# Latent heads: the next head's scores ahead of this head's transposes, with two probability buffers; first loads, first down block and program end reordered

## The reference

```python
for l in range(DEPTH):                        # DEPTH = 2, D_MODEL = 1024
    n = rms_norm(x, attn_norm[l])
    h = n @ w_in[l]                           # 1472 columns: group A q k v, latent q, latent kv, rope key
    q_b = (rms_norm(h[q_lora], q_norm) @ w_uq).reshape(b, s, 4, 128 + 64)
    ckv, k_rope = rms_norm(h[kv], kv_norm), rope(h[kr])
    o_a = window_attention(q_a, k_a, v_a, sinks)             # group A: 8 heads, banded
    # group B, 4 latent heads; prompt, chunk-causal over 512 keys
    s = (q_nope_h . (ckv @ w_uk_h) + q_rope_h . k_rope) * scale
    o_h = softmax(mask(s)) @ (ckv @ w_uv_h)
    # the samples attend in latent space to 256 cached latents + 16 new ones
    x = x + concat(rms_norm(o_a), rms_norm(o_b)) @ w_out
    n = rms_norm(x, ffn_norm[l])
    x = x + (silu(n @ w_gate) * (n @ w_up)) @ w_down         # D_FF = 2816 = 22 tiles of 128
y = rms_norm(x, final_norm)
```

## Time and profile before

| | us |
|---|---|
| runs, median of 3 | 1589.42 (1586.65 to 1590.17) |
| the profiled execution | 1587.84 |
| its span, first to last instruction | 1586.5 |
| PE busy / DVE busy / ACT busy / POOL busy | 1473.4 / 943.1 / 667.4 / 167.4 |
| PE waits in the latent heads, layer 0, 186 to 264 us | 14.5 |
| mean granted TensorE clock over the span | 0.965 of full |

### The profile page before, as it was taken

The page is one execution under the profiler, slowest core; times in us unless marked ns, Lnnn a source line. Parts: engine busy times, 40 slices in busy tenths (PEclk is TensorE's granted clock), DMA queues, the critical chain, the costliest instruction groups (busy, mean ns, idle before and its releaser), DMA issues.

```text
span 1586.5 us, 23820 instructions
## 1 busy us (share of the span) xinstructions
PE 1473.4 (93%) x9510; PEld 1386.9 (87%) x9510; DVE 943.1 (59%) x1579; ACT 667.4 (42%) x1302; POOL 167.4 (11%) x114
## 2 busy tenths in 40 slices
PE   5987888899999999999999788899999999999997
PEld 4877666799899999999988666668998999999997
DVE  5267535475878467467534754446677765765763
ACT  4255535333335235235334464353343542532543
POOL 3024200220000000000111440011100000000004
PEclk9998989799999999999999888998999999999999
DMA  3222012023222322321222201121312231332212
GB/s 142 81 80 69 14 48 63 27 80 93 78 75 94 89 74 81 97 64 54 75 81 90 75 25 40 42 69 44 103 54 87 81 110 51 99 98 64 88 41 100
DMA packets 150605, 115.74 MB, mean 73 GB/s; under 512 B 14656, under 2 KB 142912, under 8 KB 150464
## 3 DMA queue, kind: packets, MB, share of 16 engines
q1 hardware_dynamic: 150496, 114.23, 23.7%
HBM read 109.43 MB, written 6.62 MB: 73 GB/s over the span
## 4 chain that ended last, share of the span: by engine, by line
PE 75%; DVE 12%; ACT 6%; issue 3%; POOL 2%; DMA 1%; SPq 0%; ACTq 0%; DVEq 0%; POOLq 0%
PE ps L524 28%; PE ps L1086 9%; PE ps L1085 9%; PE ps L1087 9%; PE ps L571 2%; PE ps L573 2%; PE ps L572 2%; ACT whi L1152 1%; DVE wlo L1600 1%; PE ps L885 1%; PE ps L911 1%; PE ps L798 1%; PE ps L872 1%; DMA wraw<-w_uq 1%; PE ps L693 1%
## 5 line engine op out<-in xcount | busy, mean ns | idle before, releaser
L1600 DVE TENSOR_TENSOR wlo<-wraw,whi 128x1024 fp32r<-128x1024 f32 (+2 forms) x120 | 127.3, 1061 | 221.2 <-ACT whi L1152 220.9
L1152 ACT ACTIVATE whi<-wraw 128x1024 fp32r<-128x1024 f32 (+2 forms) x120 | 109.1, 914 | 260.1 <-PE ps L524 164.9
L1086 PE MATMUL ps<-tl,ringh 128*128 128x320 f32 x576 | 177.8, 309 | 0.0
L1087 PE MATMUL ps<-tth,ringl 128*128 128x320 f32 x576 | 177.5, 308 | 0.0
L1085 PE MATMUL ps<-tth,ringh 128*128 128x320 f32 x576 | 177.0, 307 | 0.0
L524 PE MATMUL ps<-hh,whi 128*128 128x320 f32 x704 | 161.1, 310 | 6.5 <-DVE hl L1928 3.5
L524 PE MATMUL ps<-hh,wlo 128*128 128x320 f32 x704 | 160.4, 309 | 0.0
L524 PE MATMUL ps<-hl,whi 128*128 128x320 f32 x704 | 160.3, 309 | 0.0
L1086 PE MATMUL ps<-tbl,ringh 128*128 128x320 f32 x432 | 133.5, 309 | 0.0
L1087 PE MATMUL ps<-tbh,ringl 128*128 128x320 f32 x432 | 133.4, 309 | 0.0
L1085 PE MATMUL ps<-tbh,ringh 128*128 128x320 f32 x432 | 133.4, 309 | 0.0
(11 more groups left out here) (368 smaller groups left out, 3345.0 us busy)
## 6 DMA issues: line engine op xcount, KB each, us to landing
raw_gate<-w_gate SPq DMA_DIRECT2D x18, 1024.0 KB, 5.3
raw_up<-w_up SPq DMA_DIRECT2D x18, 1024.0 KB, 5.4
wraw<-w_down SPq DMA_DIRECT2D x48, 384.0 KB, 3.5
wraw<-w_in SPq DMA_DIRECT2D x16, 512.0 KB, 3.8
wraw<-w_out SPq DMA_DIRECT2D x32, 128.0 KB, 2.9
wraw<-w_out SPq DMA_DIRECT2D x16, 256.0 KB, 3.1
wraw<-w_gate SPq DMA_DIRECT2D x8, 512.0 KB, 3.9
wraw<-w_up SPq DMA_DIRECT2D x8, 512.0 KB, 4.0
```

The costliest lines, as they stand in the source:

```text
L1086: mm(o, wh[:, c, :], xl[:, c, :], start=False, stop=False, skip_group_check=True)
L1087: ins = mm(o, wl[:, c, :], xh[:, c, :], start=False, stop=c == KH - 1, skip_group_check=True)
L1152: run(whi[:, slot(s, unit_width(u))], wraw[:, slot(s, unit_width(u))], ACT.Copy).then_inc(unit_hi.sem, 1)
L1600: vec.tensor_tensor(wlo[:, w], wraw[:, w], whi[:, w], ALU.subtract).then_inc(unit_lo.sem, 1)
```

## The change

Six parts, with names as in the code:

1. **Heads.** A second probability buffer pm1; heads use pm and pm1 by turns. Scores take three banks, blocks 0 and 1 sharing bank 0, and the four blocks become three groups (`rows_of`), so that p_max needs one reduction for two blocks. PE's order for each h is now p_scores(h+1), p_turn(h), k_nope(h+2), q_nope(h+2), p_values(h). The transposes go to three banks (4; 5; 3, in the last head 7), so no copy stands between two of them.
2. **Before the heads.** k_nope(1) comes ahead of p_scores(0); the samples' transposes take four banks; latent_values stands right behind them; the splitting of w_uv moves to the input stage (after unit 10), its load behind unit 9's.
3. **Start.** Of kc only the identity is loaded first (64 KB), the rest after unit 1 of w_in; SP's wait for n_lo, with gv and the masks, comes after unit 4. The high and low parts of unit 0 are made before the last token tile is copied out, those of unit 1 after chunk 2, and the masks' copy leaves the start on DVE.
4. **First down block.** wraw, whi and wlo are cut so that four of its 512-column units fit; up to six are loaded and split ahead. PE does rows 0 to 2 of d = 0 and of d = 1, and only then row 3 of both. Some of DVE's preparation comes later. SP waits, before each of these loads, until the one before in the same semaphore has landed.
5. **Layer boundary.** The wait for n_lo moves in both layers; the rest of the layers' seam stays.
6. **End.** The gain is multiplied into yT ahead of the transposes (ACT for chunks 0 to 6, in place of nh; DVE for chunk 7), ten transposes come ahead of the last unit, the last squares are added by PE in PSUM, and ACT and DVE write the scaled tiles at once. fg, its load and POOL's seven instructions go.

```diff
@@ SP
-        sp.dma_start(kc[:, :], a["consts"][:, 0:K_W]).then_inc(consts_in.sem, 16)
+        sp.dma_start(kc[:, 0:P], a["consts"][:, 0:P]).then_inc(consts_in.sem, 16)
...
+                if U_DOWN < u < U_DOWN + NC_:
+                    sp.wait_ge(raw_in[s].sem, raw_value(s, l, u) - 16)
...
-                if u == 1:
+                if u == 9:
+                    sp.dma_start(uv[:, :, :], w_uv[l]).then_inc(uv_in.sem, 16)
+                if u == 1 and l == 0:
+                    sp.dma_start(kc[:, P:K_W], a["consts"][:, P:K_W]).then_inc(tables_in.sem, 16)
+                if u == 4:
                     if l == 0:
                         sp.dma_start(mask_in[:, :], a["consts"][:, K_W:]).then_inc(win_in.sem, 16)
                     sp.wait_ge(n_lo.sem, n_lo.at(l, 1))
@@ PE, the heads
             for h in range(BH):
                 if h + 1 < BH:
-                    k_nope(h + 1)
-                p_turn(h)
-                if h + 1 < BH:
                     p_scores(h + 1)
                 else:
+                    pe.wait_ge(p_e.sem, p_e.at(l, 3 * BH - 1))
                     sample_queries()
-                    c_turn(0)
-                if h == 0:
-                    latent_values()
-                p_values(h)
+                p_turn(h)
                 if h + 2 < BH:
+                    k_nope(h + 2)
+                    pe.wait_ge(p_tact.sem, p_tact.at(l, h + 1))
+                    pe.wait_ge(p_tdve.sem, p_tdve.at(l, 2 * h + 2))
                     q_nope(h + 2)
                 if h == BH - 1:
-                    c_turn(1)
+                    c_turn(0)
+                p_values(h)
+            c_turn(1)
@@ PE, block 0
+                    if blk == 0 and d == 1:
+                        down_rows(blk, d, range(TILES[blk] - 1))
+                        for both in range(2):
+                            down_rows(blk, both, [TILES[blk] - 1]).then_inc(unit_used.sem, 1)
+                        continue
@@ ACT, the exponentials
-            def p_exps(h):
-                for i in range(TS):
+            def p_exp(h, k):
+                act.wait_ge(p_nm.sem, p_nm.at(l, 3 * h + k + 1))
+                if h >= 2 and k == 0:
+                    act.wait_ge(p_t.sem, p_t.at(l, 3 * h - 3))
+                for i in rows_of[k]:
@@ DVE, the end
-            vec.scalar_tensor_tensor(out=yout[:, t, 512:D], in0=ps[:, 2 * (t % 3) + 1, :], scalar=rs[:, t:t + 1], in1=fg[:, 512:D],
-                                     op0=ALU.mult, op1=ALU.mult).then_inc(y_dve.sem, 1)
+            vec.tensor_scalar(yout[:, t, 512:D], ps[:, (6 if t == 3 else 2 * (t % 4)) + 1, :], rs[:, t:t + 1], None, ALU.mult).then_inc(y_dve.sem, 1)
@@ POOL, the end
-        for t in range(NT):
-            pool.wait_ge(y_scaled.sem, t + 1)
-            add(yout[:, t, 0:512], yout[:, t, 0:512], fg[:, 0:512], ALU.mult).then_inc(y_pool.sem, 1)
```

More of the change, by code:

```diff
@@ L400, in load @@
                     parts, k, w = src.shape
-                    dst = wraw[part0:part0 + parts, s * SLOT + first * width:s * SLOT + (first + k) * width]
+                    c0 = unit_cols(u).start + first * width
+                    dst = wraw[part0:part0 + parts, c0:c0 + k * width]
                     dst = dst.rearrange("p (k n) -> p k n", k=k)[:, :, 0:w]
@@ L485, in _ @@
                 first, end = GROUPS_OF[blk]
-                load_down(blk, 0)
-                load_down(blk, 1)
+                ahead = 2 if blk else 6
+                for d in range(ahead):
+                    load_down(blk, d)
                 if blk == 0:
@@ L515, in unit_parts @@
         def unit_parts(u, n):
-            s = unit_slot(u)
-            return [w[:, slot(s, unit_width(u))].rearrange("p (k n) -> p k n", n=n) for w in (whi, wlo)]
+            return [w[:, unit_cols(u)].rearrange("p (k n) -> p k n", n=n) for w in (whi, wlo)]
         def by_weights(outs, w, k, cols, xh, xl, first, last):
@@ L532, in sums, with y_turn @@
             ins.then_inc(stat_sum.sem, 1)
+        def y_turn(t, chunks):
+            banks = 6 if t == 3 else 2 * (t % 4)
+            for c in chunks:
+                ins = turn(ps[:, banks + c // 4, (c % 4) * P:(c % 4 + 1) * P], yT[:, c, tok(t)], ident)
+            return ins
         def spread(n, bank):
@@ L873, in p_turn @@
+                for bank, rows in ((4, (0,)), (5, (1, 3)), (3 if h < BH - 1 else 7, (2,))):
+                    for j in rows:
+                        o = 384 if j == 3 else 0
+                        for i in range(j, TS):
+                            ins = turn(ps[:, bank, o + (i - j) * P:o + (i - j + 1) * P],
+                                       pms[h % 2][:, POFF[i] + j * P:POFF[i] + (j + 1) * P], ident)
                     ins.then_inc(p_t.sem, 1)
             def p_values(h):
-                pe.wait_ge(p_tact.sem, p_tact.at(l, 2 * h + 2))
+                pe.wait_ge(p_tact.sem, p_tact.at(l, h + 1))
@@ new lines, in _ @@
+        for t in range(NT):
+            mm(ps[:, 7, 500 + t:501 + t], ssq[:, tok(t)], one, start=True, stop=False, skip_group_check=True)
+            if t == 0:
+                pe.wait_ge(sq_new.sem, sq_new.at(DEPTH, 1))
+            ins = mm(ps[:, 7, 500 + t:501 + t], sq[:, 1, tok(t)], one, start=False, stop=True, skip_group_check=True)
+        ins.then_inc(stat_sum.sem, 1)
+        pe.wait_ge(stat_sd.sem, stat_sd.at(DEPTH, 1))
+        y_turn(3, range(NC_)).then_inc(tile_turned.sem, 1)
+        pe.wait_ge(y_scaled.sem, 1)
@@ L1151, in weight_hi @@
             act.wait_ge(unit_used.sem, unit_used.at(l, used_before(u)))
-            run(whi[:, slot(s, unit_width(u))], wraw[:, slot(s, unit_width(u))], ACT.Copy).then_inc(unit_hi.sem, 1)
+            run(whi[:, unit_cols(u)], wraw[:, unit_cols(u)], ACT.Copy).then_inc(unit_hi.sem, 1)
         act.wait_ge(consts_in.sem, 32)
@@ L1207, in _ @@
                         run(v[:, :, :], hm[:, :, C_V:C_Q], ACT.Copy).then_inc(v_new.sem, 1)
+                if u == 10:
+                    act.wait_ge(uv_in.sem, uv_in.at(l, 16))
+                    run(uvh[:, :, :], uv[:, :, :], ACT.Copy).then_inc(uv_hi.sem, 1)
                 if u == 8:
@@ L1380, in _ @@
                 if h + 1 < BH:
[L1381 to L1390 removed]
+                    p_exp(h + 1, 0)
+                    p_exp(h + 1, 1)
                 else:
@@ L1685, in _ @@
                     latents_norm()
+                if u == 10:
+                    dve.wait_ge(uv_hi.sem, uv_hi.at(l, 1))
+                    vec.tensor_tensor(uvl[:, :, :], uv[:, :, :], uvh[:, :, :], ALU.subtract).then_inc(uv_lo.sem, 1)
             def keys_out_dve(t):
```

363 lines of the change are left out of this document (204 added, 159 removed).

## The result

The changed kernel takes 1533.95 us (median of four runs, 1531.5 to 1534.86), the kernel before 1588.74 us on the same chip: a ratio of 0.9654, 95% interval 0.9637 to 0.967. It is 55 us faster where 44 were forecast, and lies a hair under the stated range (1534 to 1562). The profiled execution has a span of 1532.6 us, so the two traces differ by 53.9 us.

A forecast was written before the change was run, and what follows sets the result against it. PE, busy 1473.4 of 1586.5 us, was taken as the bound, with only gaps and half-clock stretches to win: heads 31.2, start 6.3, block 0 4.6, end 2.1, sum 44.2; from 1587.84 to 1543.6, plus 1.6 for the median: 1545 us, range 1534 to 1562.

The forecast's parts named there:

- the clock of the heads: Latent heads: of 7.0 and 8.6 us lost to the clock, 1.9 and 3.5 won, 5.1 a layer left in place.
- Rival B: Clock stays up through the latent stage (+10 us) and unit 2 is ready in time (+3): 1533 us; chance 0.15.
- rival C: Gaps between short groups keep PE at half clock through the latent stage, 51 us a layer more: 1647 us; chance 0.02.
- Heads, gaps: Latent stage: PE's gaps fall from 14.5 to 1.6 us, 12.9 a layer; a middle head takes 11.5 us.
- Start: Input stage: unit 2 lands early, PE resumes at 34.35 instead of 40.65 us, still at half clock; gain 6.3 us.
- Block 0: First down block: three gaps, 3.3 us a layer, go; waits of 0.3 and 0.7 us remain; gain 4.6 us in all.
- End: Final stores: reciprocal 0.7 us earlier, first store moves from 1578.70 to about 1576.6 us; gain 2.1 us.
- A: Heads close only halfway, each waiting 1.5 us for qnl or p_norm; they give 18 us, not 31: 1558 us; chance 0.20.
- D: Scores of h+1 can't run ahead; only start, block 0 and end give, 13 us: 1576 us; chance 0.06.

The follow-up runs named there:

- values_early: Changed kernel with the samples' values straight behind the samples' transposes, ahead of latent_values; 1534.64 us.
- before_k: Kernel before with one move, k_nope(1) ahead of the scores of head 0; 1583.43 us, ratio 0.9976 to the kernel before.
- one_buf: Changed kernel with one buffer of probabilities instead of two, PE's order unchanged; 1542.86 us, ratio 0.973 to the kernel before.
- end_old: Changed kernel with the old end (gain on POOL and DVE, all transposes behind the last unit); 1534.83 us, ratio 0.9661 to the kernel before.
- end3: Changed kernel, ten transposes moved behind the last unit, sums over chunks 0 to 6 right behind its product, one start for the bank; 1531.49 us, ratio 0.9641.
- end2: Changed kernel, ten transposes moved behind the last unit, sums over chunks 0 to 6 right behind its product, a start per column; 1530.66 us, ratio 0.9653.

## Why the prediction was right and wrong

**The step that failed** is the one on the clock of the heads: "The small matmuls stay and a small gap ahead of the first scores stays, so I leave these 5.1 in place and count only the others as won." All of it was won: 15.0 us by the granted clock (which is given to two digits, so some 0.5 us either way in each layer) instead of 5.4. That is about the whole miss of 9.7, 53.9 against 44.2; the errors of the other terms about cancel. The scores of head 0 ran at full clock behind the 0.8 us that stayed, and so did the samples' values. I had taken the 64-column matmuls for the cause, since they stood at 0.56 in the earlier trace rows. The same matmuls ran at 1.00 in the changed kernel, at 1.00 behind a wait of 1.35 us (values_early), and at both levels in one execution of before_k. They were where the fall showed, not what made it. What went with every fall in this stage was standing still: by the granted clock, one wait of 2.2 us put back cost 1.7 us in layer 0 and nothing in layer 1, two cost 3.5 and 1.7, and the row of waits of the kernel before 6.9 and 8.0. But not every standstill took the clock, and by what rule some do stays open.

Rival B had this mechanism, at a chance of 0.15 and 1533 us, and the argument against it was the same misreading. That the time fell so near its 1533 is in part luck: of its 13 us, the 3 for unit 2 in time did not come (PE still waited 2.37 us), and in their place stand the 1.8 us that block 0 gave beyond its forecast and the 1.6 us that had been added for the median, which now lies 0.3 us under the profiled execution.

A second misreading stands beside it: "1.00 in the middle heads of before" is true of the head in the earlier trace rows, but in layer 1 one ran at 0.51 for 3.4 us (before_k, above). It was used against rival C. Rival C's own condition is off too: 22 us a layer are lost by spending 44 us at half clock, not 22.

**Heads, gaps** (25.8 forecast, 24.1 measured): the mechanism was right and the size near. The 0.8 ahead of the scores and the copies of ptm ahead of p_values(2) (0.94) came where they were forecast; 0.29 ahead of p_values(3) had been missed. A middle head takes 10.97 us and not 11.5, since it had been sized by PE's busy time in a stretch with pauses.

The Trainium skill (TensorE: Matmul & The Clock Gate, section A second HAM failure mode: psum-queue depth-cycling) tells of a kernel in which frequent short pauses between groups of matmuls made the clock swing between its levels. The kernel before agrees in part (0.93 and 0.92 over its stages, with the row of waits). The changed middle heads have no pause (10.97 of 10.97 us busy) and can't show it, and one_buf has waits of 0.7, 0.7 and 2.1 us at 1.00.

**Start** (6.3, 7.1): the mechanism held, step by step. nl(7) ended at 33.8 and not at 32.4, wlo(2) at 34.96 and not at 34.3, so unit 2 began 5.7 us earlier; the rest of the 7.1 came behind it, where the kernel before restarted at half clock. "The restart at half clock stays" was wrong for this trace: behind 2.37 us PE started at full clock, behind 7.73 and 6.61 at half. It was right for end_old and end3, at half behind 2.04 and 2.11 us.

**Block 0** (4.6, 6.4): the mechanism was right, the size low. Of the two residual waits of 0.3 and 0.7 only one of 0.32 came, and PE's busy time fell by 0.3 us a layer with the waits, at a clock of 1.00 in both.

**End** (2.1, 0.7): the sum left out that the squares of chunk 7, now added by PE, double the sums, from 1.17 us to 2.3. The reciprocal came 0.5 us later and not 0.7 earlier, counted from the last low part; only POOL's hand-over on the way to the store was won.

**Rivals** A, C and D are refuted: no wait for qnl or pm, no half clock in the stage, and the scores do run ahead.

## What to carry to other kernels

Count what a row of standstills costs twice: once as gaps, and once as clock over the matmuls behind them. Read the clock in every layer or repetition of a stage, not in one. When a change takes away most of the standstills of a stage, count the clock loss of the whole stage as part of what can be won, and give the case in which it all comes back a fair chance. Don't read the kind of instruction that runs slow as the cause of the slowness; look at what the engine did before it. And where single swaps are worth 1 to 3 us, measure the stage between two instructions that no version changes, since the rest of the program moves by as much from run to run.

## What the runs showed of the hardware

Nearly equal rows of waits gave different clocks in the two layers of one execution (before_k: 1.00 in 202 to 208 us, 0.50 in 971 to 979). By what rule is left open: the runs vary the waits, not where they fall. And two ends that differ in one flag: with a start for each of five columns in one PSUM bank before the second set of matmuls (end2), part of the first set was missing from the sums; with one start for the bank (end3) the sums were whole. The Trainium skill (PSUM — Partial Sum Buffer, section The four PSUM rules) says that an opening matmul clears the marks of what has been written over the whole bank, so that the next matmul onto the other columns overwrites. The two runs agree. That it was the first four columns which lost their first set is worked out from that rule; no run shows the columns.
